# Attention by pairs of heads: row-packed scores, one pass for mask and maximum, division at the output

## The reference

```python
def attend(q, k, v, mask, sink):
    s = einsum('bqkgd,bskd->bkgqs', q, k) * (HEAD_DIM ** -0.5)
    if mask is not None: s = where(mask, s, NEG_INF)
    if sink is not None: p = softmax(concat([s, sk]))[..., :-1]
    else: p = softmax(s)
    return einsum('bkgqs,bskd->bqkgd', p, v)
```

## Time and profile before

| what | value |
|---|---|
| median of 3 runs | 4026.54 us (4011.68 to 4033.96) |
| the profiled execution, span from first to last instruction | 4014.0 us |
| TensorE busy | 3650.9 us, 91% |
| TensorE weight loads | 1877.7 us, 47% |
| VectorE busy | 1066.1 us, 27% |
| ScalarE busy | 627.9 us, 16% |
| mean granted TensorE clock | 0.944 |
| HBM read | 547.30 MB, 137 GB/s over the span |

### The profile page before, as it was taken

One profiled execution on the slowest core, in us unless ns is written; L12 is line 12 of the kernel. 1 busy time (PEld: TensorE's weight loads), 2 busy tenths in 40 slices (PEclk: granted clock), 3 DMA queues, 4 the chain that ended last, 5 costly groups with the idle time before them and its releaser, 6 DMA issues. The chain is left out here.

```text
span 4014.0 us, 39150 instructions
## 1 busy us (share of the span) xinstructions
PE 3650.9 (91%) x15258; PEld 1877.7 (47%) x15258; DVE 1066.1 (27%) x1845; ACT 627.9 (16%) x1128; POOL 16.2 (0%) x34
## 2 busy tenths in 40 slices
PE   5999989999997899999989999999778878889998
PEld 3556555655555343433354654644422322335554
DVE  2525421531113101101043552511201001153342
ACT  2103211320002010100120321300200100111221
POOL 1000000000000000000000000000000000000000
PEclk8999998989997999999999999999799999999559
DMA  6110025013420678688812001022199899711000
GB/s 199 38 51 11 11 67 174 1 53 116 137 94 21 221 282 323 243 318 294 304 49 63 22 21 63 1 73 74 58 367 343 321 366 343 236 52 63 1 1 21
DMA packets 375362, 551.80 MB, mean 137 GB/s; under 512 B 56936, under 2 KB 170872, under 8 KB 375064
## 3 DMA queue, kind: packets, MB, share of 16 engines
q1 hardware_dynamic: 373360, 546.60, 39.0%
q0 software_dynamic: 1520, 2.81, 0.2%
q10 hardware_dynamic: 312, 0.05, 0.0%
HBM read 547.30 MB, written 2.10 MB: 137 GB/s over the span
## 5 line engine op out<-in xcount | busy, mean ns | idle before, releaser
L627 PE MATMUL ps<-hT,ring 128*128 128x512 f32 (+1 forms) x2576 | 977.8, 538 | 76.1 <-DVEq L1031 31.2
L814 PE MATMUL ps<-ring,hT 128*64 128x512 f32 x3072 | 710.1, 600 | 99.7 <-DMA ring<-in_w_e_up 43.6
L627 PEld LDWEIGHTS ps<-hT,ring 128*128 128x128 f32 x2576 | 492.9, 193 | 550.6 <-issue 502.3
L814 PEld LDWEIGHTS ps<-ring,hT 128*64 128x64 f32 x3072 | 200.3, 136 | 586.7 <-issue 382.9
L627 PE MATMUL ps<-obuf,ring 128*128 128x512 f32 (+1 forms) x704 | 271.8, 538 | 1.0 <-DVE obuf L1457 1.0
L733 PE MATMUL ps<-probT,vbuf 128*64 128x128 f32 x1744 | 269.1, 303 | 0.0
L708 PE MATMUL ps<-kbuf,qbuf 64*128 64x256 f32 (+3 forms) x640 | 266.1, 517 | 1.6 <-DVEq L1031 1.6
L733 PEld LDWEIGHTS ps<-probT,vbuf 128*64 128x64 f32 x1744 | 205.6, 149 | 47.7 <-issue 47.3
L1046 ACT ACTIVATE prob<-ps,nms 128x768 f32<-128x768 f32 (+5 forms) x224 | 151.5, 676 | 470.4 <-DVE nms L1434 235.0
L1567 DVE SCALAR_TENSOR_TENSOR xT<-ps,mod,xT 128x512 f32<-128x512 f32 x96 | 63.5, 662 | 523.1 <-PE ps L882 281.1
L627 PEld LDWEIGHTS ps<-obuf,ring 128*128 128x128 f32 x704 | 132.9, 191 | 132.8 <-issue 128.9
(11 more groups left out here) (173 smaller groups left out, 2340.4 us busy)
## 6 DMA issues: line engine op xcount, KB each, us to landing
ring<-in_w_e_gate SPq DMA_DIRECT2D x256, 512.0 KB, 7.5
ring<-in_w_e_up SPq DMA_DIRECT2D x256, 512.0 KB, 8.4
ring<-in_w_e_down SPq DMA_DIRECT2D x256, 512.0 KB, 7.5
ring<-in_w_in SPq DMA_DIRECT2D x51, 1024.0 KB, 5.3
ring<-in_w_ada SPq DMA_DIRECT2D x48, 1024.0 KB, 11.5
ring<-in_w_branch SPq DMA_DIRECT2D x12, 1024.0 KB, 5.2
ring<-in_w_out SPq DMA_DIRECT2D x12, 1024.0 KB, 5.2
ring<-in_w_in SPq DMA_DIRECT2D x40, 256.0 KB, 4.8
```

The costliest lines, as they stand in the source:

```text
L627: mm = pe.matmul(ps[:, b + a:b + e], lhs[:, k, :], rhs[:, k, a:e], start=k == 0, stop=k == nk - 1)
L814: mm = pe.matmul(ps[e * CX:(e + 1) * CX, b + pair * 512:b + (pair + 1) * 512], lhs[:, k, s0:s0 + CX], expert_dst(slot, e)[:, k % 2, :], st ...
```

## The change

The unit becomes a pair of heads, one in the partitions 0 to 63 of the queries and keys and one in 64 to 127.

- **Scores** of both heads are computed one after the other for each segment, the one into slot 0 and the other into slot 1. The mask products are gone.
- **Mask and maximum**: one VectorE instruction per head (`tensor_tensor_reduce`) reads the scores in PSUM, scales them by -1/8, adds the mask (a column of zeros repeated where there is none), writes the result into SBUF and gives the minimum as well. The exponentials (`E`) are computed in place in SBUF.
- **Division** moves behind the value products: once for a block of 8 heads (`Q`) VectorE inverts the 8 sums and spreads each over 64 columns of `sq`, TensorE turns these four tiles over (`R`), and the outputs are multiplied by that (`O`, on VectorE). In S and D, `R` multiplies the gate instead. Sinks are exponentiated once a block (`K`).
- **Turns** (`T`) of both heads go in groups of two tiles to two PSUM banks that alternate (`TBANK`), with a copy of up to 512 columns each: groups 0 and 2 by ScalarE, group 1 by VectorE. Copies go to `merged` or `hT`.
- **Value products** (`V`) take two pairs at once: 256 columns move for each 64 columns of values, the two heads of a pair alternating between the columns 0 to 63 and 64 to 127 of the array. In D, with values of its own for each head, 128 columns move. The products of two pairs are spread over two steps.
- **Order of the layer**: the convolution moves from before attention A, and the third gate with its branch from before attention B, both to behind attention B. After `qa3`, and after `qb3`, nothing is left in `pipelined` but the `hs` and `rot` jobs.
- Rows of `w_branch` and `w_out_2`, and columns of the gate `g2a`, are loaded in the order of the pairs, with two to four DMAs in place of one. The masks of the second block are loaded by GpSimd ahead of it, with the tables of the rotation.

The core of the diff:

```diff
         def attention_order(key):
-            for s in range(n + 2):
-                if 0 <= s - 1 < n: order.append(("N", key, s - 1))
-                if s < n: order.append(("S", key, s))
...
+            for s in range(n + 3):
+                banks = (len(units[s - 1]["tiles"]) + 1) // 2 if 1 <= s <= n else 0
+                if s < n:
+                    order.append(("S", key, s))
+                if s % 4 == 0 and 4 <= s <= n:
+                    order.append(("Q", key, s // 4 - 1))
+                if banks:
+                    order.append(("T", key, s - 1, 0))
+                if s < n:
+                    order.append(("E", key, s))
+                    if s % 4 == 3 and key in SINK:
+                        order.append(("K", key, s // 4))
+                if banks > 1:
+                    order.append(("T", key, s - 1, 1))
+                if s % 4 == 1 and s >= 5:
+                    order.append(("R", key, s // 4 - 1))
+                if s >= 3:
+                    h, part = (s - 3) // 2, (s - 3) % 2
+                    if h < n // 2:
+                        order.append(("V", key, h, part))
+                        if part and h % 2:
+                            order.append(("O", key, h // 2))
+                if banks > 2:
+                    order.append(("T", key, s - 1, 2))
...
-            order += pipelined([("qk", l, f"qb{j}") for j in range(4)] + gates[2])
-            order += attention_order((l, 1)) + gates[0] + gates[1]
+            order += pipelined([("qk", l, f"qb{j}") for j in range(4)])
+            order += attention_order((l, 1)) + conv + gates[2] + gates[0] + gates[1]
...
 TensorE
+                    b = [begin(j + (a,), a) for a in range(2)]
                     for n, (c0, w, k0) in enumerate(u["segs"]):
+                        for a in range(2):
+                            r = slice(a * HD, (a + 1) * HD)
+                            mm = pe.matmul(ps[:, b[a] + c0:b[a] + c0 + w], q[r, u["g"], u["q0"]:u["q0"] + P],
+                                           k[r, u["kj"], k0:k0 + w], start=True, stop=True)
...
+                    steps = [(g, m, a) for g in (range(2) if own else (None,)) for m in range(len(tiles)) for a in range(2)]
+                    cut = len(steps) // 4 * 2 or 1
+                    for g, m, a in steps[cut:] if late else steps[:cut]:
+                        r = slice(a * HD, (a + 1) * HD)
...
+                            out_, exp_, col = ps[r, b:b + 2 * P], exps[:, m, a].rearrange("p g t -> p (g t)"), u["vcols"][a]
+                        mm = pe.matmul(out_, v(tiles[m], col), exp_, start=m == 0, stop=m == len(tiles) - 1,
+                                       tile_position=(0, a * HD))
...
 VectorE
-                    V.do(v.tensor_reduce(mxn[:, h:h + 1], ps[:, b + u["lo"]:b + u["hi"]], AX.X, ALU.max, negate=True))
...
+                        V.do(v.tensor_tensor_reduce(scored(j[2], a, u), ps[:, b + u["lo"]:b + u["hi"]], mask, -SCALE, least,
+                                                    ALU.add, ALU.min, stats(nms, t, u, a)), s_ready, j + (a,))
+                        V.release(j + (a,))
```

More of the change, by code:

```diff
@@ L206, in units_first @@
             for st, i in streams:
[L207 to L224, removed]
+                q0, mask = (i * P if st == "x" else NX + i * P), None
+                if st == "c":
+                    segs, lo, hi, tiles = [(0, NC, NX)], 0, NC, [4, 5]
+                elif br == 0:
+                    segs, lo, hi, tiles = [(0, NX, 0), (NX, NC, NX)], 0, NT, list(range(6))
+                elif i == 0:
+                    segs, lo, hi, tiles, mask = [(512, 2 * P, 0), (768, NC, NX)], 512, 1024, [0, 1, 4, 5], 3 * P
+                else:
+                    n = min(3, NX // P + 1 - i)
+                    segs, lo, hi, mask = [(256, NC, NX), (512, n * P, (i - 1) * P)], 256, 512 + n * P, 0
+                    tiles = [4, 5] + [i - 1 + m for m in range(n)]
+                for g in range(4):
+                    units.append(dict(q0=q0, t=q0 // P, g=g, heads=(g, 4 + g), kj=br,
+                                      segs=segs, lo=lo, hi=hi, tiles=tiles, mask=mask, vcols=(0, HD)))
             return units
@@ L229, in units_second @@
             for i in range(NX // P):
[L230 to L241, removed]
+                a = max(0, i - 1) if br == 0 else 0
+                n = (i - a + 1) * P
+                for g in range(4):
+                    heads = (g, 4 + g) if br == 0 else (2 * g, 2 * g + 1)
+                    units.append(dict(q0=i * P, t=i, g=g, heads=heads, kj=0 if br == 0 else g, segs=[(0, n, a * P)],
+                                      lo=0, hi=n, tiles=list(range(a, i + 1)),
+                                      mask=M_BAND + 2 * P - n if br == 0 else M_DIL + 4 * P - n,
+                                      vcols=(0, HD) if br == 0 else (P + heads[0] * HD, P + heads[1] * HD)))
             return units
@@ L582, in begin @@
                     slot, turn[0] = turn[0], (turn[0] + 1) % 3
+                if slot == 2 and in_banks[0]:
+                    for r in range(2):
+                        pe.wait_ge(tb_done[r].sem, bank_at[r])
+                    in_banks[0] = False
                 n = used[slot]
```

331 lines of the change are left out of this document (194 added, 137 removed).

## The result

| | before | after |
|---|---|---|
| median | 4020.9 us (4011.7 to 4034.0, 4 runs) | 3744.6 us (3742.1 to 3751.2, 4 runs) |
| span of the profiled execution | 4014.0 | 3749.4 |
| mean granted clock | 0.944 | 0.951 |

What follows compares the result with a forecast made beforehand. TensorE was taken as the bound, ScalarE's loop at 512 and 256. Attentions save 280 us, new waits cost 69: 211 off the span of 4014.0 gives 3803, with 12.5 around it 3815 us; range 3750 to 3925.

Steps and rivals of the forecast that it cites:

- attentions: The six attentions: forecast to fall from 807 to 527 us, 280 saved.
- order: New order of layers 0 and 1: waits ahead of four attentions, forecast to cost 69 us.
- the 3.5 us taken for every 256-wide step: Step of a 256-wide pair of heads: ScalarE's loop about 3.0 us at full clock, 3.5 at half; 3.5 taken.
- S and D at 0.5 and together near 125: Expected sign in the profile after: attentions S and D at half clock, 59 and 66 us.
- the loop: ScalarE's chain at 256: turns, copy, two exponentials, next turn; about 3.0 us at full clock, 3.5 at half.
- all warm: Rival: S, D and context parts at full clock, 38 us more saved, 3777; chance 0.09, shared with fewer stalls.
- Filling and draining three stages costs 12 us an attention: Added to the steps of each attention: 12 us in A0 to B1, 8 in S, 6 in D.
- a start at half clock: After the new waits TensorE starts cold: 5 us added in each of A0, B0, A1, B1.
- 0.96 for the pass: Fused VectorE pass at 768 columns: 0.96 us taken, between bounds of 0.95 and 4.95.
- the overlap of row halves: Both heads' scores run at once, 1.28 us a pair at 768; rival without overlap: 104 us back, 3919, chance 0.12.
- Loads at nothing: Split weight loads land during attentions and cost nothing; if uncovered, about 5.2 us each.
- ScalarE's step: Rival: ScalarE sets the step, 5.3 us at 768 and 4.0 at 256; 54 us back, 3869, chance 0.13.

Runs made afterwards that it cites:

- the serial kernel by pairs: The changed kernel with both heads' scores from partitions 0 to 63, value products in two blocks, and mask products back on TensorE in S and D: 3943.7 us.

## Why the prediction was wrong

The span was forecast at 3803 and came out at 3749.4, 54 us lower. By the terms of the sum: attentions 83 us too dear, order 3 too cheap, experts 19 and the rest 7 not foreseen; 83 - 3 - 19 - 7 = 54. That the miss is 54 and not 83 is luck. Two steps failed, each worth some 40 of the 83 us.

- **The clock of before, carried into a changed program**: the 3.5 us taken for every 256-wide step, the sum's value "at half", and "S and D at 0.5 and together near 125". S was back at 1.00 after 18 us; D was at 0.50 once more, for 10 us near its start, and then at 1.00 to its end. A 256-wide step took 2.66 at the full clock. At half clock two of them in S took 3.14 and 4.10 (their scores start at 3591.12, 3594.26 and 3598.36), so 3.5 was about right for a level that was wrong: of the 0.84 between 3.5 and 2.66, 0.50 is the level, and 0.34 the loop, which was summed at 3.0. In A0 the 3.5 even went against the earlier trace rows, where that part ran at 1.00. All this is 27 us in S and D (125 against 97.6, of which about 4 are the filling of S), and 8 x 0.84 = 6.7 us in each of A0 and B0, 13. The rival *all warm* had 50 + 50 us for S and D, with 0.09 of the chance.
- **"Filling and draining three stages costs 12 us an attention"**, and 5 more for a start at half clock. A0 took 103.1 - 16 x 4.80 - 8 x 2.66 = 5.0 beyond its steps, A1 84.6 - 76.8 = 7.8, and with my 3.5 for 512 and the 4.17 measured for 640, B0 took 8.3 and B1 6.5: 27.6 instead of 68, 40 us. Filling cost next to nothing: in A0 the first sixteen steps took 76.9 us (scores start at 200.54, and those of the seventeenth step at 277.41), against 16 x 4.80 = 76.8. The first two ran mostly at half clock (5.40 and 5.29 us), but value products come only with the fourth. What is left is draining: the end came 7.0 to 11.9 us behind the last scores, the last step's own time among it. The 640-wide steps give the last 2.
- **Right**: 4.80 at 768; 0.96 for the pass (0.958, and 0.08 to read the minimum); the overlap of row halves, and about the price if it failed (104 forecast, 115 in the run, in which longer cold stretches are); the waits, 72 for 69. Loads at nothing fits the run with whole loads (3737.9); the load of the masks, `K` and `Q` have no run of their own.
- **ScalarE's step** was wrong at 768, where it waits for TensorE. At 256 ScalarE does set the step; in the timeline of S TensorE waits for its exponentials:

```profile
3618.17 0.63 PE L785 MATMUL ps<-con,prob 128*128 128x128 f32 x4 [0.82 <-ACT prob L1132]
...
3618.88 0.59 ACT L1238 COPY hT<-ps 128x512 f32<-128x512 f32 x1 [0.81 <-ACT prob L1132]
...
3619.50 0.51 ACT L1132 ACTIVATE prob<-prob,nms 128x256 f32<-128x256 f32 x1
...
3620.13 0.51 ACT L1132 ACTIVATE prob<-prob,nms 128x256 f32<-128x256 f32 x1
...
3620.83 0.63 PE L785 MATMUL ps<-con,prob 128*128 128x128 f32 x4 [0.38 <-ACT prob L1132]
```

  Turn to copy 0.71, copy 0.62, exponentials 0.63 and 0.70: 2.66. The loop was the right one, summed at 3.0, and then priced at half clock, 3.5.
- **Not settled**: why S stayed at 0.50 before. Shown is what alone doesn't change it: taking out the mask products, those of the first eight heads or all, or the new order; and a kernel by pairs is warm there without the overlaps, with the mask products, and at a busy share as high. What all warm kernels share and no cold one has is the rest of the change: pairs of heads, with half as many changes between kinds of product, the fused pass, exponentials from SBUF, and the division behind the values. These were not separated.

## What to carry to other kernels

Packing small products into halves of the array saved nearly a whole product of two, for rows and for columns (1.8 and 1.9 times); for columns it needs instructions that alternate between the halves, and rows were run in no other way. Ask of an old order what it covered before moving it: 72 of the 363 us went back to waits that other projections had filled, and moving the values into them bought 18. Don't carry a stretch's granted clock into a new program; price such a stretch at both levels and let the range hold both.

## What was not expected of the hardware

- The same instructions can be granted different clocks in different executions. A0's context heads ran at 1.00 in the earlier trace rows; in the kernel before with padded constants, where nothing of A0 was changed, that stretch shows

```profile
425.00:457.00 32.00, 30.56 (x121) 17.80 (x119) 16.50 (x54) 11.14 (x34) 0.00 (x0) 0.68 0.00 1
```

  and A0 took 169.5 us instead of 159.3, while B0 took 169.6 instead of 177.0. Each is 7 to 10 us, beside 22 by which runs of the kernel before differ. Whether the padding had a part in it isn't shown.
- Busy is not warm: 1.00 with 35.9 of 36 us busy in the serial kernel by pairs, and in S before

```profile
3755.00:3838.00 83.00, 81.82 (x222) 47.51 (x223) 35.00 (x124) 23.01 (x77) 0.00 (x0) 0.50 0.00 1
```

- The rate of the expert weights, 334 to 345 GB/s, differs between kernels that differ only in an attention over long before; one execution of each was profiled.
